# A two-layer mixer kernel: loops written out, Exps one head ahead, a new order at the program's head

## The chip, the cores and the metric

The kernel runs on one core of a Trainium2 chip. The metric is the device time of one execution, in microseconds (us), median of the runs shown. TensorE is called PE, its weight loads PEld, VectorE DVE, ScalarE ACT, GpSimd POOL; SP is the sync engine, which here only starts transfers.

## The reference

Two transformer-like blocks in float32 over 512 latent tokens (and 256 context tokens in the first), model width 2048:

```python
# first block
shift, scale, gate = split(silu(c) @ w_ada + b_ada, 3)
h  = rmsnorm(x, norm_g) * (1 + scale) + shift        # the same for ctx with c_ctx
u  = h @ w_in;  uc = hc @ w_in
ya = gdn_mixer(...)     # gated delta rule, 8 heads of 128, both directions
yb = rwkv_mixer(...)    # RWKV-7 recurrence, 16 heads of 64, both directions
x  = x + gate * (concat(ya, yb) @ w_out) -> rmsnorm
# delta rule, chunks of 64 (the kernel takes two as one unit of 128), state starts at zero
v_new = u_i - wk_i @ state
o_i   = q_i @ state + attn_i @ v_new
state = state * exp(gl_i) + k_i.T @ v_new
# second block: adaLN, attention in a window of 128, conformer convolution, w_out_2, layer norm
```

## The kernel before, in words

The program is a row of phases (PHASES), each with its own semaphores and with a barrier of all engines between two of them.

- phase_mod: the modulation c @ w_ada as 8 column groups of 512, two per round (groups), four rounds of 64 recorded matmuls each; the weights come in 1 MB slices through 8 slots that SP fills. Beside it the sum of squares of x and ctx: ACT squares hT (L253), PE sums over partitions with a matrix of ones (L289, L290), a pair of matmuls for each of 16 slices. Round 0 stands before the sums, rounds 1 to 3 behind them in a loop. DVE copies each round's result (L306, L308) and scales hT (L315).
- phase_gates: decay and beta of the delta rule, 32 columns; a long chain on DVE behind 32 matmuls.
- phase_split: ACT rounds hT to the multiplier's format (h_high, L1045), DVE makes the remainder (h_low, L1052).
- phase_proj: all columns of w_in.
- phase_rwkv: 8 pairs of heads. In each pair a scan over 2 x 6 steps with the preparation of the next half pair filled in between the steps (prepare), the finish of the pair before (heads_out) and the weighted sum of later w_ada slices on DVE (later, L2293, L2296). SP loops over pairs 0 to 6, PE and ACT over pairs 1 to 6, DVE over pairs 2 to 6. A loop's waits compare against a value that registers hold.
- phase_gdn: 8 heads. scan(m) does six steps j of head m; fill(m, n), n = 0 to 17, three per step, puts in the finish of head m-1 (norm), the second part of the preparation of head m+1 (invert) and the first part of head m+2 (start). start(a, 0): DVE takes differences of gates (L779, L782), ACT makes Relu and Exp of them (L707 to L710); start(a, 1): PE forms k k^T (L599), DVE multiplies it by those Exps (L788). In a step PE multiplies the state (L665), DVE subtracts (L867), PE multiplies by the inverse (L671), ACT copies (SA, L746), PE makes the state's increment (L675), DVE adds it (L873); steps 2 to 5 give an output (L683, L684, L885).
- phase_out and phase_two: output projection and the second block.

What each engine does is written out by hand in the order in which it runs; there is no scheduler. In phase_gdn, step 0 of each head starts from two memsets:

```python
for d in range(2):
    dve.memset(St[0][:, d], 0.0).then_inc(S["g_s"], 1)
```

Of the kernel before, what the change touches and what calls it, by code (L numbers as in the profile page):

```python
# [69 lines left out]
def program(nc, io, out):  # L70
    ctx = ExitStack()
    with ctx:
# [20 lines left out]
        mixers, halves_of_h = ctx.enter_context(ExitStack()), ctx.enter_context(ExitStack())  # L93
        first, work = ctx.enter_context(ExitStack()), ctx.enter_context(ExitStack())
# [71 lines left out]
        for f, prefixes in phases:  # L166
            at[0] = 0
            if prefixes == "s":
                first.close()
                env["high"] = sb("h_high", [P, KT, TOK], F32R, scope=halves_of_h)  # L170
                env["low"] = sb("h_low", [P, KT, TOK], F32R, scope=halves_of_h)
            if prefixes == "pq":
                mixers.close()
# [24 lines left out]
def phase_mod(nc, e):  # L198
# [10 lines left out]
    sq = carve(2, TOK)  # L209
    rstd = carve(TOK)  # L210
# [11 lines left out]
    with nc.Block() as block:  # L222
# [21 lines left out]
        def _(act):  # L244
            act.dma_start(hT[:, :, 0:LAT], io["xT"]).then_inc(S["a_x"], 16)
            act.dma_start(hT[:, :, LAT:TOK], io["ctxT"]).then_inc(S["a_x"], 16)
            act.wait_ge(S["a_par"], 48)
            act.activation(csg[:], pr("c", 3 * KT).rearrange("p (k s) -> p k s", s=3), ACT.Sigmoid).then_inc(S["a_sig"], 1)
            act.wait_ge(S["a_x"], 32)
            for k in range(KT):  # L250
                if k >= 2:
                    act.wait_ge(S["a_ss"], k - 1)
                act.activation(sq[:, k % 2], hT[:, k], ACT.Square).then_inc(S["a_sq"], 1)  # L253

            act.wait_ge(S["a_ss"], KT)
# [11 lines left out]
        def _(pe):  # L267
            pe.wait_ge(S["a_par"], 48)
            pe.wait_ge(S["a_cs"], 1)

            def groups(i):
# [9 lines left out]
                for b in range(2):  # L281
                    pe.wait_ge(S["a_row"], 1 + i * 2 + b + 1)
                    for n in range(4):
# [2889 lines left out]
```

## Time and profile before

| | |
|---|---|
| median of 3 runs | 4146.47 us (4146.44 to 4146.88) |
| profiled execution, its own time | 4150.37 us |
| its span, first to last instruction | 4148.6 us |
| mean granted TensorE clock | 0.921 |
| busy | PE 85%, PEld 71%, DVE 53%, ACT 25%, POOL 20% |
| DMA | 467.29 MB, mean 113 GB/s |

The span is the profiled execution's; its own time is 1.8 us more, and the median of the runs is 3.9 us below that. Busy shares are means over phases with different limits, so the chain in each phase has to be read by itself.

### The profile page before, as it was taken

The numbers are of one execution on the slowest core, as the hardware profiler recorded it, in microseconds if no ns is written. First come the engines' busy times: TensorE is split into PE (matmuls) and PEld (weight loads), VectorE is DVE, ScalarE is ACT, GpSimd is POOL, SyncE is SP. The second block draws the span as 40 slices with busy tenths as digits, with TensorE's granted clock in tenths as the row PEclk, the third lists the DMA queues.
The fourth block names the chain that finished last, engine by engine and source line by source line (L and its number), as shares of the span: only waits on it lengthen the run. The fifth ranks groups of instructions, "written<-read, shape, count | busy, mean of one in ns | idle before, by whom it ended". The sixth has DMA issues, their size and how long they took to land. (4 is left out here: it accounts for less than half of the span.)

```text
span 4148.6 us, 53353 instructions
## 1 busy us (share of the span) xinstructions
PE 3525.3 (85%) x19810; PEld 2930.3 (71%) x19810; DVE 2202.7 (53%) x4087; ACT 1042.4 (25%) x1716; POOL 825.8 (20%) x589
## 2 busy tenths in 40 slices
PE   6849999989999588888888778887797989887897
PEld 2138888878888487887788668776676777665484
DVE  0252655555545366666666646665103789993102
ACT  1122554543333112221221212221002221212102
POOL 0000000000000011111111100000575665563273
PEclk9969999999999799999999868888899999998899
DMA  6411434345455455555555333321523221121221
GB/s 270 132 44 64 138 121 148 121 136 174 151 167 167 94 125 127 127 116 118 123 124 119 107 94 107 103 81 66 191 81 117 71 71 61 66 71 46 101 96 66
DMA packets 409792, 467.29 MB, mean 113 GB/s; under 512 B 266544, under 2 KB 310416, under 8 KB 403040
## 3 DMA queue, kind: packets, MB, share of 16 engines
q1 hardware_dynamic: 377536, 379.20, 30.9%
q0 software_dynamic: 20480, 67.13, 5.4%
q10 hardware_dynamic: 11552, 17.95, 1.2%
q8 instruction: 144, 2.36, 0.2%
q14 instruction: 80, 0.66, 0.1%
HBM read 382.80 MB, written 83.99 MB: 113 GB/s over the span
## 5 line engine op out<-in xcount | busy, mean ns | idle before, releaser
L953 PE MATMUL pjl<-high,w_high 128*128 128x512 f32 x912 | 374.8, 411 | 48.4 <-DVE low L2519 16.3
L934 POOL TENSOR_TENSOR w_high<-ring_o,cst 128x1024 fp32r<-128x1024 f32 x152 | 302.2, 1988 | 491.9 <-PE pjl L955 343.0
L936 POOL TENSOR_TENSOR w_low<-ring_o,w_high 128x1024 fp32r<-128x1024 f32 x152 | 380.8, 2505 | 11.9
L954 PE MATMUL pjl<-low,w_high 128*128 128x512 f32 x912 | 365.9, 401 | 0.0
L955 PE MATMUL pjl<-high,w_low 128*128 128x512 f32 x912 | 364.1, 399 | 0.0
L2892 DVE SCALAR_TENSOR_TENSOR arena<-arena,par 128x512 f32<-128x512 f32 x232 | 312.5, 1347 | 7.4
L1931 POOL DMA_DIRECT2D arena_r<-in_w_ada x256 | 137.4, 537 | 857.0 <-DVE arena_r L2296 754.4
L953 PEld LDWEIGHTS pjl<-high,w_high 128*128 128x128 f32 x912 | 177.8, 195 | 103.6 <-issue 53.0
L1090 PE MATMUL pjl<-h_high,wh_in 128*128 128x512 f32 x544 | 214.8, 395 | 24.2 <-DVE wl_in L1109 24.2
L1109 DVE TENSOR_TENSOR wl_in<-ring,wh_in 128x1024 fp32r<-128x1024 f32 x136 | 164.2, 1221 | 132.6 <-ACT wh_in L1102 132.6
L1090 PE MATMUL xu<-h_high,wh_in 128*128 128x512 f32 x544 | 220.2, 405 | 0.0
L1925 POOL MEMSET unused<- 128x1 f32 x3 | 0.2, 98 | 1101.5 <-POOLq L194 1101.5
L1090 PE MATMUL xu<-h_high,wl_in 128*128 128x512 f32 x544 | 214.9, 395 | 0.0
L1090 PE MATMUL pjl<-h_high,wl_in 128*128 128x512 f32 x544 | 214.4, 394 | 0.0
L1090 PE MATMUL xu<-h_low,wh_in 128*128 128x512 f32 x544 | 213.9, 393 | 0.0
L1090 PE MATMUL pjl<-h_low,wh_in 128*128 128x512 f32 x544 | 213.5, 393 | 0.0
L955 PEld LDWEIGHTS pjl<-high,w_low 128*128 128x128 f32 x912 | 177.7, 195 | 38.8
L954 PEld LDWEIGHTS pjl<-low,w_high 128*128 128x128 f32 x912 | 177.8, 195 | 38.0 <-issue 1.9
L2296 DVE SCALAR_TENSOR_TENSOR arena_r<-arena_r,csk 128x512 f32 (+1 forms) x240 | 179.7, 749 | 13.4 <-DMA arena_r<-in_w_ada 2.3
L2088 PE MATMUL xu<-arena_r 128*128 128x128 f32 x384 | 90.5, 321 | 105.5 <-DVE arena_r L2316 78.0
L1102 ACT ACTIVATE wh_in<-ring 128x1024 fp32r<-128x1024 f32 x136 | 142.6, 1054 | 100.4 <-DMA ring<-in_w_lr 58.6
L2170 ACT ACTIVATE arena_r<-tp 128x384 f32<-128x384 f32 (+1 forms) x96 | 57.4, 598 | 402.8 <-PE tp L2047 402.0
(454 smaller groups left out, 7920.4 us busy)
## 6 DMA issues: line engine op xcount, KB each, us to landing
ring<-in_w_lr SPq DMA_DIRECT2D x136, 512.0 KB, 3.7
arena_r<-in_w_ada POOLq DMA_DIRECT2D x256, 256.0 KB, 3.2
arena<-in_w_ada SPq DMA_DIRECT2D x32, 1024.0 KB, 7.4
ring_o<-in_w_out SPq DMA_DIRECT2D x64, 512.0 KB, 3.8
ring_o<-in_w SPq DMA_DIRECT2D x64, 512.0 KB, 3.7
arena_r<-rk_d SPq DMA_DIRECT2D x128, 192.0 KB, 5.1
rk_d<-arena_p SPq DMA_DIRECT2D x72, 192.0 KB, 1.9
arena_p<-gate_rows SPq DMA_DIRECT2D x32, 386.0 KB, 6.1
```

Source lines behind the costliest of these rows:

```text
L934: pool.tensor_tensor(h, w, one, ALU.mult).then_inc(S[done + "h"], 1)
L936: pool.tensor_tensor(l, w, h.bitcast(F32), ALU.subtract).then_inc(w_used, 1)
L953: pe.matmul(lat, wh[:, c], ah, start=kk == 0, stop=False)
L954: pe.matmul(lat, wh[:, c], al, start=False, stop=False)
L955: last = pe.matmul(lat, wl[:, c], ah, start=False, stop=kk == KT - 1)
L1090: last = pe.matmul(lat, w[:, s, k], a[:, kk, 0:LAT], start=first, stop=final)
L1102: act.activation(e["wh"][:, n % RING], e["ring2"][:, n % 2], ACT.Copy).then_inc(S["p_hi"], 1)
L1109: dve.tensor_tensor(e["wl"][:, n % RING], e["ring2"][:, n % 2], e["wh"][:, n % RING].bitcast(F32), ALU.subtract).then_inc(S["p_split"], 1)
L1931: pool.dma_start(late[:, x % LATE], io["w_ada"][8 + x // 16, :, x % 16]).then_inc(S[f"r_lw{x % LATE}"], 16)
L2088: pe.matmul(xu[d][:, 0:P], LC[hh][:, d, u], twice(V[hh][:, d, u]), start=True, stop=False)
L2296: dve.scalar_tensor_tensor(a, late[:, k % LATE], c, a, ALU.mult, ALU.add).then_inc(S["r_lu"], 1)
L2892: link(dve.scalar_tensor_tensor(ca[:], x[:, o:o + LAT], w[:, o:o + 1], ca[:], ALU.mult, ALU.add))
```

## The change

- phase_mod: SP asks for par first, then four weight slices, then cst and rows; ACT makes the sigmoid of c before it starts the transfers of x and ctx. Rounds 0 and 1 of the modulation both stand ahead of the sums. The 16 squares are added up on DVE (adds, between the copies of round 1), and PE multiplies the total by ones once.
- phase_split is gone; its 16 ACT and 16 DVE instructions stand in phase_gates, ACT's behind the first Exp, DVE's behind the memsets.
- phase_rwkv: the loops of SP, PE, ACT and DVE are written out, so that addresses and waits are constants.
- phase_gdn: step 0 has no product with the state, no subtraction and no memset; its new state is a copy. Step 5 makes no new state. start(m+3, 0) is in scan m, on DVE at n = 15 and on ACT at n = 16, in place of start(m+2, 0) at n = 0; start(2, 0) stands ahead of the first scan.
- The block transfers (blocks_out to inverse_in) are as they were.

```diff
@@ phase_mod
             sp.dma_start(par[:], io["par"]).then_inc(S["a_par"], 16)
-            sp.dma_start(cst[:], io["cst"]).then_inc(S["a_par"], 16)
-            sp.dma_start(rows[:], io["rows"]).then_inc(S["a_par"], 16)
             for s in range(SLOTS):
...
+                if s == 3:
+                    sp.dma_start(cst[:], io["cst"]).then_inc(S["a_cst"], 16)
+                    sp.dma_start(rows[:], io["rows"]).then_inc(S["a_rows"], 16)
...
+            act.wait_ge(S["a_par"], 16)
+            act.activation(csg[:], pr("c", 3 * KT).rearrange("p (k s) -> p k s", s=3), ACT.Sigmoid).then_inc(S["a_sig"], 1)
             act.dma_start(hT[:, :, 0:LAT], io["xT"]).then_inc(S["a_x"], 16)
             act.dma_start(hT[:, :, LAT:TOK], io["ctxT"]).then_inc(S["a_x"], 16)
-            act.wait_ge(S["a_par"], 48)
-            act.activation(csg[:], pr("c", 3 * KT).rearrange("p (k s) -> p k s", s=3), ACT.Sigmoid).then_inc(S["a_sig"], 1)
+            act.wait_ge(S["a_rows"], 16)
...
-                    act.wait_ge(S["a_ss"], k - 1)
+                    act.wait_ge(S["a_add"], k - 1)
...
-            groups(0)
-            for k in range(KT):
-                pe.wait_ge(S["a_sq"], k + 1)
-                pe.matmul(ssl[:, 0:LAT], ones, sq[:, k % 2, 0:LAT], start=k == 0, stop=k == KT - 1)
-                pe.matmul(ssc[:, 0:CTX], ones, sq[:, k % 2, LAT:TOK], start=k == 0, stop=k == KT - 1).then_inc(S["a_ss"], 1)
-            with pe.Fori(1, GROUPS // 2) as i:
+            pe.wait_ge(S["a_zero"], 1)
+            groups(0, True)
+            groups(1)
+            pe.wait_ge(S["a_add"], KT)
+            pe.matmul(ssl[:, 0:LAT], ones, sums[:, 0:LAT], start=True, stop=True)
+            pe.matmul(ssc[:, 0:CTX], ones, sums[:, LAT:TOK], start=True, stop=True).then_inc(S["a_ss"], 1)
+            with pe.Fori(2, GROUPS // 2) as i:
                 groups(i)
...
+            def adds(k0, k1):
+
+                for k in range(k0, k1):
+                    dve.wait_ge(S["a_sq"], k + 1)
+                    if k:
+                        dve.wait_ge(S["a_add"], k)
+                        dve.tensor_tensor(sums[:], sums[:], sq[:, k % 2], ALU.add).then_inc(S["a_add"], 1)
...
                 for b in range(2):
+                    if i == 1:
+                        adds(*((0, 4), (4, KT))[b])
@@ phase_gates
+            for k in range(KT):
+                act.activation(high[:, k], hT[:, k], ACT.Copy).then_inc(S["b_h"], 1)
...
+            for k in range(KT):
+                dve.wait_ge(S["b_h"], k + 1)
+                dve.tensor_tensor(low[:, k], hT[:, k], high[:, k].bitcast(F32), ALU.subtract).then_inc(S["b_l"], 1)
+            dve.wait_ge(S["b_l"], KT)
             dve.wait_ge(S["b_y"], 2)
@@ phase_gdn, tensor: scan
-                        pe.wait_ge(S["g_s"], m * 14 + 2 * j + d + 1)
+                        if j == 0:
+                            break
+                        pe.wait_ge(S["g_s"], m * 10 + 2 * (j - 1) + d + 1)
...
-                        pe.matmul(xu[d][:, P:2 * P], TT[m % 2][:, d, G_ORDER[d][j]], W[:, d], start=True, stop=True).then_inc(S["g_sa"], 1)
+                        else:
+                            pe.wait_ge(S["g_wc"], m * 10 + 2 * (j - 1) + d + 1)
+                        pe.matmul(xu[d][:, P:2 * P], TT[m % 2][:, d, u], W[:, d] if j else bV[m % 2][:, d, u], start=True, stop=True).then_inc(S["g_sa"], 1)
...
+                        if j == UN - 1:
+                            continue
                         pe.matmul(xu[d][:, 2 * P:3 * P], KL[m % 2][:, d, G_ORDER[d][j]], SA[:, d], start=True, stop=True).then_inc(S["g_ds"], 1)
@@ phase_gdn, scalar: fill (vector: the same with n == G_EARLY, which is 15)
-                if m + 2 < GH:
+                if m + 2 < GH and n:
                     start(m + 2, n)
+                if m + 3 < GH and n == G_EARLY + 1:
+                    start(m + 3, 0)
@@ phase_gdn, vector: scan
-                if m:
-                    dve.wait_ge(S["g_s"], m * 14)
-                for d in range(2):
-                    dve.memset(St[0][:, d], 0.0).then_inc(S["g_s"], 1)
...
+                        if j == 0:
+                            dve.tensor_copy(new[:, d], xu[d][:, 2 * P:3 * P]).then_inc(S["g_s"], 1)
+                            continue
@@ phase_rwkv (PE; ACT, DVE and SP alike)
-            with pe.Fori(1, PAIRS - 1) as i:
+            for i in range(1, PAIRS - 1):
                 pair(i, True)
```

The order of instructions at three places. **PE at the program's head.** Before (the first rows, up to the loop over rounds 1 to 3, of which L278 is the body; the rows of L289 and L290 come 16 times), and then the change, where the modulation's lines are L283 and L291 and the sums' L297 and L298:

```order
L278 MATMUL xu<-arena 3x512 x32
L284 MATMUL tp<-cst,arena 128x128 x8
L289 MATMUL pjl<-arena,cst 128x512
L290 MATMUL pjc<-arena,cst 128x256
```

```order
L283 MATMUL xu<-arena 3x512 x32
L291 MATMUL tp<-cst,arena 128x128 x8
L283 MATMUL xu<-arena 3x512 x32
L291 MATMUL tp<-cst,arena 128x128 x8
L297 MATMUL pjl<-arena,cst 128x512
L298 MATMUL pjc<-arena,cst 128x256
```

A whole round has moved ahead of the sums, and the sums are one pair of matmuls.

**ACT in phase_gdn, from step 5 of one head to the preparation filled into the next.** Before: Square of norm (L726), Relu and Exps of start (L707 to L710), the copy SA of step 0 (L746), Sqrt of norm (L729), T's copies (L720).

```order
L746 ACTIVATE arena_r<-xu 128x128 x4
L726 ACTIVATE arena_r<-arena_r 128x512
L707 ACTIVATE arena_r<-arena_r 128x1536
L709 ACT_TABLE_LOAD
L709 ACTIVATE arena_r<-arena_r 128x1536
L710 ACTIVATE arena_r<-arena_r 128x12
L746 ACTIVATE arena_r<-xu 128x128 x2
L729 ACT_TABLE_LOAD
L729 ACTIVATE arena_r<-pjl,arena_r 128x512
L720 ACTIVATE arena_r<-tp 128x768 x2
```

Now (L743 to L746 are Relu and Exps, L762 the Square, L784 the copy, L765 the Sqrt, L756 T's copies):

```order
L784 ACTIVATE arena_r<-xu 128x128 x4
L743 ACTIVATE arena_r<-arena_r 128x1536
L745 ACT_TABLE_LOAD
L745 ACTIVATE arena_r<-arena_r 128x1536
L746 ACTIVATE arena_r<-arena_r 128x12
L762 ACTIVATE arena_r<-arena_r 128x512
L784 ACTIVATE arena_r<-xu 128x128 x2
L765 ACT_TABLE_LOAD
L765 ACTIVATE arena_r<-pjl,arena_r 128x512
L756 ACTIVATE arena_r<-tp 128x768 x2
```

The Exps stand ahead of the Square, and they are those of the head after the one that they were for.

**DVE at the same place.** Before: the last state (L873) and output (L885) of a head, the memsets (L861), step 0 (L867), invert (L811), the gates' differences (L779, L782), k k^T times the Exps (L788), the new state.

```order
L867 TENSOR_TENSOR arena_r<-arena_r,xu 128x128 x2
L873 SCALAR_TENSOR_TENSOR arena_r<-arena_r,xu 128x128 x2
L885 TENSOR_TENSOR arena_r<-arena_r,pjl 128x128 x2
L861 MEMSET arena_r 128x128 x2
L867 TENSOR_TENSOR arena_r<-arena_r,xu 128x128 x2
L811 TENSOR_TENSOR arena_r<-arena_r 128x768 x2
L779 TENSOR_TENSOR arena_r<-arena_r,gc 128x6x64 x2
L782 TENSOR_TENSOR arena_r<-arena_r,gc 128x6
L779 TENSOR_TENSOR arena_r<-arena_r,gc 128x6x64 x2
L782 TENSOR_TENSOR arena_r<-arena_r,gc 128x6
L788 TENSOR_TENSOR arena_r<-tp,arena_r 128x768 x2
L873 SCALAR_TENSOR_TENSOR arena_r<-arena_r,xu 128x128 x2
```

Now (L908 is the subtraction, L820 and L823 the differences, L931 the output, L852 invert, L829 the product with the Exps, L917 the copy that makes the state):

```order
L908 TENSOR_TENSOR arena_r<-arena_r,xu 128x128 x2
L820 TENSOR_TENSOR arena_r<-arena_r,gc 128x6x64 x2
L823 TENSOR_TENSOR arena_r<-arena_r,gc 128x6
L820 TENSOR_TENSOR arena_r<-arena_r,gc 128x6x64 x2
L823 TENSOR_TENSOR arena_r<-arena_r,gc 128x6
L931 TENSOR_TENSOR arena_r<-arena_r,pjl 128x128 x2
L852 TENSOR_TENSOR arena_r<-arena_r 128x768 x2
L829 TENSOR_TENSOR arena_r<-tp,arena_r 128x768 x2
L917 COPY arena_r<-xu 128x128 x2
```

The four differences have moved from behind step 0 of a head to step 5 of the head before.

## Rows read from the trace of the kernel before

**Rows 1.** Timeline of phase_mod: start us, us, engine, line, operation [idle before it].
```profile
1.47 17.54 ACTq L246 DMA_DIRECT2D hT<-in_ctxT  x1
20.93 29.65 PE L278 MATMUL xu<-arena 128*3 128x512 f32 x64 [20.93 <-DVE arena L299]
...
63.50 1.58 ACT L253 ACTIVATE arena<-hT 128x768 f32<-128x768 f32 x2 [42.91 <-DMA hT<-in_ctxT]
...
87.70 27.63 PE L278 MATMUL xu<-arena 128*3 128x512 f32 x64
...
173.24 0.66 PE L284 MATMUL tp<-cst,arena 128*128 128x128 f32 x4
```
**Rows 2.** DMA, 0 to 30 us: packets, MB, share; then issues, KB, us to landing.
```profile
q1 hardware_dynamic: 1261, 8.51, 70.3%
q10 hardware_dynamic: 1447, 2.96, 25.7%
...
par<-in_par SPq DMA_DIRECT2D x1, 402.0 KB, 3.2
```
**Rows 3.** Timeline of phase_gates, phase_split and the start of phase_proj.
```profile
224.15 0.55 DVE L420 TENSOR_SCALAR arena<-arena 16x772 f32<-16x772 f32 x1 [34.72 <-ACT arena L400]
...
260.15 11.84 ACT L1045 ACTIVATE h_high<-hT 128x768 fp32r<-128x768 f32 x16 [3.85 <-PEq L194]
261.02 13.99 DVE L1052 TENSOR_TENSOR h_low<-hT,h_high 128x768 fp32r<-128x768 f32 x16 [1.85 <-ACT h_high L1045]
...
275.91 0.26 POOL L1199 MEMSET unused<- 128x1 f32 x6 [275.06 <-POOLq L194]
```
**Rows 4.** DVE timeline, the first instruction of pairs 0, 1, 2, 3, 6, 7.
```profile
1442.04 0.19 DVE L2357 MEMSET arena_r<- 128x64 f32 x2
...
1558.02 0.18 DVE L2357 MEMSET arena_r<- 128x64 f32 x2
...
1676.88 0.19 DVE L2357 MEMSET arena_r<- 128x64 f32 x2
...
1799.77 0.19 DVE L2357 MEMSET arena_r<- 128x64 f32 x2 [3.25 <-issue]
...
2165.35 0.19 DVE L2357 MEMSET arena_r<- 128x64 f32 x2 [3.23 <-issue]
...
2283.76 0.18 DVE L2357 MEMSET arena_r<- 128x64 f32 x2
```
**Rows 5.** ACT timeline in phase_gdn, the start of a head.
```profile
2708.85 0.63 ACT L726 ACTIVATE arena_r<-arena_r 128x512 f32<-128x512 f32 x1 [2.88 <-DVE arena_r L885]
2713.95 1.48 ACT L707 ACTIVATE arena_r<-arena_r 128x1536 f32<-128x1536 f32 x1 [4.47 <-DVE arena_r L782]
...
2718.24 0.42 ACT L746 ACTIVATE arena_r<-xu 128x128 f32<-128x128 f32 x2
```
**Rows 6.** DVE timeline there, from step 5 of the head before.
```profile
2704.12 0.48 DVE L867 TENSOR_TENSOR arena_r<-arena_r,xu 128x128 f32<-128x128 f32 x2
...
2708.33 0.48 DVE L885 TENSOR_TENSOR arena_r<-arena_r,pjl 128x128 f32<-128x128 f32 x2 [1.12 <-PE pjl L684]
...
2711.81 1.02 DVE L779 TENSOR_TENSOR arena_r<-arena_r,gc 128x384 f32<-128x384 f32 x2
...
2720.10 0.60 DVE L873 SCALAR_TENSOR_TENSOR arena_r<-arena_r,xu 128x128 f32<-128x128 f32 x2
```
**Rows 7.** PE timeline there.
```profile
2710.57 1.02 PE L644 MATMUL pjl<-arena_r,cst 128*128 128x512 f32 x2
2711.43 2.84 PE L599 MATMUL tp<-arena_r 128*128 128x128 f32 x24
2718.55 1.22 PE L675 MATMUL xu<-arena_r 128*128 128x128 f32 x4 [4.28 <-ACT arena_r L746]
2720.24 2.08 PE L604 MATMUL tp<-arena_r 128*128 128x128 f32 x8 [0.47 <-DVE arena_r L788]
```
**Rows 8.** Window early in the head before: length, busy by engine, PEclk, DMA share, GB/s.
```profile
2664.00:2668.00 4.00, 3.53 (x16) 3.24 (x16) 3.56 (x7) 1.83 (x2) 0.00 (x0) 0.50 0.29 43
```

More of the change, by code:

```diff
@@ L93, in program @@
         mixers, halves_of_h = ctx.enter_context(ExitStack()), ctx.enter_context(ExitStack())
+        gates_work = ctx.enter_context(ExitStack())
         first, work = ctx.enter_context(ExitStack()), ctx.enter_context(ExitStack())
@@ L209, in phase_mod @@
     sq = carve(2, TOK)
+    sums = carve(TOK)
     rstd = carve(TOK)
@@ L267, in _, with groups @@
         def _(pe):
-            pe.wait_ge(S["a_par"], 48)
             pe.wait_ge(S["a_cs"], 1)
-            def groups(i):
+            def groups(i, first=False):
                 for b in range(2):
@@ L282, in groups @@
                     pe.wait_ge(S["a_row"], 1 + i * 2 + b + 1)
+                    if first and b == 0:
+                        pe.wait_ge(S["a_cst"], 16)
                     for n in range(4):
@@ L295, in _ @@
         def _(dve):
-            dve.memset(modr[:], 0.0).then_inc(e["w_used"], RING)
+            dve.memset(modr[:], 0.0).then_inc(S["a_zero"], 1)
+            dve.wait_ge(S["a_zero"], 1)
+            dve.memset(sums[:], 0.0).then_inc(e["w_used"], RING)
             dve.memset(eps[:], 1e-6).then_inc(S["a_eps"], 1)
@@ L350, in phase_gates @@
     ea = carve(1)
-    gc = e["gc"]
+    gc, high, low = e["gc"], e["high"], e["low"]
     R = slice(0, 16)
@@ L479 @@
 G_TURNED, G_DONE = 6, 10
+G_EARLY = 15
 def phase_gdn(nc, e):
@@ L755, in _ @@
                 invert(0, n)
+            start(2, 0)
             for m in range(GH):
@@ L850, in fill @@
                     invert(m + 1, n)
-                if m + 2 < GH:
+                if m + 2 < GH and n:
                     start(m + 2, n)
+                if m + 3 < GH and n == G_EARLY:
+                    start(m + 3, 0)
                 if m + 1 < GH and n >= 3:
@@ L865, in scan @@
                     for d in range(2):
-                        dve.wait_ge(S["g_w"], m * 12 + 2 * j + d + 1)
+                        if j == 0:
+                            break
+                        dve.wait_ge(S["g_w"], m * 10 + 2 * (j - 1) + d + 1)
                         dve.tensor_tensor(W[:, d], bV[m % 2][:, d, G_ORDER[d][j]], xu[d][:, 0:P], ALU.subtract).then_inc(S["g_wc"], 1)
@@ L871, in scan @@
                         u = G_ORDER[d][j]
-                        dve.wait_ge(S["g_ds"], m * 12 + 2 * j + d + 1)
+                        if j == UN - 1:
+                            break
+                        dve.wait_ge(S["g_ds"], m * 10 + 2 * j + d + 1)
+                        if j == 0:
+                            dve.tensor_copy(new[:, d], xu[d][:, 2 * P:3 * P]).then_inc(S["g_s"], 1)
+                            continue
                         dve.scalar_tensor_tensor(new[:, d], old[:, d], egl[m % 2][:, d, u:u + 1], xu[d][:, 2 * P:3 * P],
@@ L897, in _ @@
                 invert(0, n) if n >= 3 else None
+            start(2, 0)
             dve.wait_ge(S["g_sh"], 1)
@@ L1035, in step_blocks @@
     dve.tensor_tensor(z[:, k + 1:16, 0:w], z[:, k + 1:16, 0:w], t, ALU.subtract).then_inc(S[q + "_z"], 1)
-def phase_split(nc, e):
-    hT, high, low, S = e["hT"], e["high"], e["low"], e["S"]
-    with nc.Block() as block:
-        @block.scalar
-        def _(act):
-            for k in range(KT):
-                act.activation(high[:, k], hT[:, k], ACT.Copy).then_inc(S["s_h"], 1)
-            act.wait_ge(S["s_h"], KT)
-        @block.vector
-        def _(dve):
-            for k in range(KT):
-                dve.wait_ge(S["s_h"], k + 1)
-                dve.tensor_tensor(low[:, k], hT[:, k], high[:, k].bitcast(F32), ALU.subtract).then_inc(S["s_l"], 1)
-            dve.wait_ge(S["s_l"], KT)
 def r_slots(d, hh):
@@ L1983, in _ @@
             load_a(0, 1)
-            with sp.Fori(0, PAIRS - 1) as i:
+            for i in range(PAIRS - 1):
                 blocks_there(i * 2 + 1)
@@ L2213, in _ @@
             pair(0, True, True)
-            with act.Fori(1, PAIRS - 1) as i:
+            for i in range(1, PAIRS - 1):
                 pair(i, True)
@@ L2285, in later @@
             def later(i, hh, n):
-                g, which = i * 2 + hh, 0 if isinstance(i, int) and i < 2 else 2
+                g, which = i * 2 + hh, 0 if i < 2 else 2
                 at = sum(LATER.get(q, 0) for q in range(n))
@@ L2375, in _ @@
             pair(0, True, True)
-            pair(1, True)
-            done = n_[0]
-            with dve.Fori(2, PAIRS - 1) as i:
-                n_[0] = 0
-                base[0] = done + (i - 2) * io["DV_R"]
+            for i in range(1, PAIRS - 1):
                 pair(i, True)
-                e["counts"]["DV_R"] = n_[0]
-            n_[0] = 0
-            base[0] = done + (PAIRS - 3) * io["DV_R"]
             pair(PAIRS - 1, False)
@@ L3170 @@
 ARENA = 32584
+GATES = 11264
 WORK, CORE = 14608, 49440
```

25 lines of the change are left out of this document (15 added, 10 removed).

## The prediction

> **What bounds the kernel now.** I read the page first (PE 85% busy, DVE 53%), then the phases one by one, since the change touches four of them and no other. In phase_mod the timeline shows PE at work from 20.93 us, at rest from about 51, waiting for x and ctx until 63.5, in the sums until 87.7, then three rounds of modulation without a break until 173.24 [rows 1]. So PE's order sets the end, and what PE does while it waits is free. PE starts at 20.93 because the sigmoid of c stands in ACT's queue behind the start of two transfers, the second of which holds the queue for 17.54 us [rows 1]. phase_split has PE idle: 15.8 us from ACT's first rounding (260.15) to the first instruction of phase_proj (275.91) [rows 3]. In phase_rwkv the seven full pairs are read from the first DVE instruction of each [rows 4]: pair 0 takes 116.0 us (no loop but SP's, and no heads_out), pair 1 118.9 (loops on PE, ACT and SP), pair 2 122.9, pairs 3 to 5 121.9 each ((2165.35 - 1799.77) / 3), pair 6 118.4. Every start behind a jump back of DVE's loop has an idle time of 3.2 us put down to issue; pair 7, where the loop is left, has none [rows 4]. In phase_gdn a head's start is a chain: gate differences on DVE, Relu and Exps on ACT, 4.3 us (2713.95 to 2718.24), then SA, then PE, idle for 4.28 us until then [rows 5, 7], then the state at 2720.10 [rows 6]. The granted clock is then low (0.50, its level of 1.2 GHz, in [rows 8], the same place one head earlier), and 8 products take 2.08 us where 24 took 2.84 before the idle time [rows 7].
>
> **Head of the program.** par lands 3.2 us after its issue [rows 2], at about 4; with the sigmoid and one product PE could begin at 5, and the first weight slice, which shares the queue with par alone, should be there by 6. PE starts 15 us sooner. Two rounds now run before the sums; a round takes (173.24 - 87.70) / 3 = 28.5 us, so they end at 6 + 57 + 2 = 65, the 2 for a start at the low clock. The transfers bound this too: 16 slices of 1.05 MB, par, cst, x and ctx are 24.6 MB, and 11.5 MB moved in the first 30 us, some 0.4 MB per us once they run [rows 2]: 63 us. Of these bytes the ACT queue got 2.96 MB against 8.51 of SP's [rows 2], and x and ctx took from 1.47 to 63.5 [rows 1]. They start 4 us later and SP's queue stays full, so I put them at 67. The 16 squares then go at the pace of DVE's additions, 13.99 / 16 = 0.87 [rows 3] plus a hand-over, 0.95: 84. Copy, transposes and the one pair of sums at low clock take 4: round 2 starts at 88, where round 1 started at 87.7. One round is saved, 28.5, less 0.3 and less 2 for the cold start: **-26**. If the later x costs 8 us more it is -18, if SP's queue yields, -29. DVE's reciprocal and eight scalings (about 12 us) stay inside round 2.
>
> **phase_split.** 15.8 us go. Its work moves behind a wait in phase_gates: DVE stands idle 34.72 us before L420 [rows 3], and 13.99 us of subtractions one step behind 11.84 us of ACT fit in; without that cover they would cost those 14. **-16** (-15 to -16.5).
>
> **Loops written out.** The four jumps back of DVE (behind pairs 2 to 5) cost the difference between 121.9 to 122.9 and pair 6's 118.4: 3.5 to 4.5 each, 14.9 together. PE's own jumps lie mostly beside it. Here the Trainium skill speaks against the change: Advanced Engine Details and Errata, Control Flow Timing, gives a compare-and-branch some 108 ns. By that page the four would give 0.4 us and not 14.9. The idle time of 3.25 us in the trace decides. Its page Runtime: NRT & Kernel Launch, Instruction fetch mechanics, has the other rule, that a taken branch out of the loaded code stalls until the target's page is there. What is left is the register work of the waits. Pair 1, whose DVE is written out, is no faster than pair 6, whose DVE is not, so DVE's is hidden; PE's could be at most the 118.4 - 116.0 that separate pair 6 from pair 0, which also lacks heads_out. I take 118.0 for a written-out pair: (2283.76 - 1558.02) - 6 x 118.0 = **-18**; at 118.4 -15, at 116.0 -30. If a written-out stream brought stalls of its own it would be less, -12.
>
> **Delta rule.** With the rows I lay out a head's start anew. Step 5's subtraction ends at 2704.6; the differences (2711.81 to 2713.95, 2.1 us) follow at once and end at 2706.7 [rows 5, 6]. Their G was loaded long before. They stand in a gap, since step 5's state update is gone, and the output L885 is not later than its 2708.33. ACT does Relu and Exps from 2706.8 to 2711.1, and only then the Square (0.63), which PE's product with ones awaits, and behind that product stands L599, which needs 2.84 us at full clock [rows 5, 7]. So: Square done 2711.7, SA 2712.2, ones 2712.7, L599 2715.5, increment and state at 2716.6, against 2720.10: 3.5 us sooner. But PE has then been idle for some 3.5 us, against 4.28 before, and may run L599 at the low clock, about 5.5 us: state at 2719.3, 0.8 sooner. In either case the slow stretch begins 6 us earlier and ends earlier, which puts up to 6 us of PE's work back to the full level and is worth up to 3. I take 4 us for each of the heads 0 to 5, which have Exps, and 1.5 for heads 6 and 7, which lose only memset, two products and a subtraction: 24 + 3 = **-27**. Ends: 1 us each, -8; 7 us each, -45.
>
> **Sum.** -26 - 16 - 18 - 27 = -87. The profiled execution took 4150.4 us, so 4063.4; the median of the runs stands 3.9 below it: **4059.5 us**.
>
> **Rivals.**
> - *The Square behind the Exps*, 0.14: in the delta rule the wait only changes its name, PE waits for the Square instead of SA and L599 runs slow. For it: the order on ACT and the low clock after the idle time [rows 7, 8]. Against: the whole chain starts 7 us sooner. Delta rule -8: 4078.5.
> - *The clock stays up*, 0.12: the idle time becomes short enough, the slow start of every head goes. For it: one idle time of 4.28 us is all that stands ahead of the slow start [rows 7]. Against: 3.5 us of it are still there. Delta rule -45: 4041.5.
> - *Loops written out bring nothing*, 0.05: pairs wait for loads or for DVE and stay at 121. Against: pair 6 has the same work in 118.4. Without the 18: 4077.5.
> - *x and ctx starve*, 0.04: SP's queue is served far ahead of ACT's while PE eats slices earlier; round 2 starts 8 us later or more: 4067.5 and up.
> - *Slower, by code loading*, 0.02: each written-out pair stops as often as code must be fetched, 3.25 us each time [rows 4]. Six pairs must lose the other 69 us (26 + 16 + 27), which takes 69 / (6 x 3.25) = 3.5 stops in a pair; from there on the kernel is slower. With six in a pair: 4146.5 - 69 + 117 = 4194.5. Against: pair 0 stands written out on PE, ACT and DVE and shows nothing of it in its 116.0 us.
>
> **How the numbers follow.** The forecast has 0.63. Its own range, from the ends of the head and of the pairs with 3 to 6 us a head in the delta rule, is 4045 to 4073. The range of eight in ten has to reach into the first two rivals, whose centres are 4078.5 and 4041.5: 4038 to 4083. A difference from no change that a measurement can tell is 0.2%, 8 us. All cases but the last are faster by more than that: 0.97 faster, 0.01 same, 0.02 slower.
>
> **What would show it.** Right: PE's first product at 6 us and third round at 88; phase_gates unchanged in length and followed by phase_proj at once; pairs 1 to 6 all within 1 us of 118 with no idle time put down to issue at their start; PE's wait at a head's start put down to the Square, shorter than 4.28 us, and a head's period shorter by about 4. Wrong: a third round later than 92; additions that hold up round 1's copy beyond 85; pairs of different length, which would mean that loads or code set them; a head's period shorter by less than 2 or by more than 6, in which case the clock is what I misjudged.

## The result, and the profile after

| | before | after |
|---|---|---|
| median of 4 runs each, same chip | 4146.68 us (4146.44 to 4152.31) | 4082.9 us (4077.84 to 4089.93) |
| ratio | 1 | 0.9844, 95% interval 0.9827 to 0.9861 |
| profiled execution, its span | 4150.4, 4148.6 | 4083.69, 4081.7 |
| mean granted clock of PE | | 0.926 |

The kernel is 64 us faster, where 87 were forecast. The length of each phase, from its first instruction to the first one of the next phase (us), against the terms of the sum:

| | phase_mod | gates + split | phase_proj | phase_rwkv | phase_gdn | phase_out | phase_two |
|---|---|---|---|---|---|---|---|
| before | 187.3 | 87.9 | 1101.7 | 1017.6 | 498.1 | 294.8 | 960.4 |
| after | 178.2 | 72.3 | 1102.9 | 1004.4 | 472.8 | 293.7 | 956.6 |
| measured | -9.1 | -15.6 | +1.2 | -13.2 | -25.3 | -1.1 | -3.8 |
| forecast | -26 | -16 | 0 | -18 | -27 | 0 | 0 |

So one term failed by 17 us, one by 5, and two held. phase_two, which the change doesn't touch, lies between 955.7 and 960.8 in the eleven profiles of the experiments below: its 3.8 us are no effect of the change. For the small terms this table is a better measure than the medians.

**Head of the program.** PE's timeline from the start, which answers to [rows 1]:

```profile
7.92 30.19 PE L283 MATMUL xu<-arena 128*3 128x512 f32 x64 [7.92 <-DMA arena<-in_w_ada]
...
39.47 27.63 PE L283 MATMUL xu<-arena 128*3 128x512 f32 x64
89.97 1.11 PE L291 MATMUL tp<-cst,arena 128*128 128x128 f32 x4 [22.87 <-DVE arena L329]
103.11 1.11 PE L291 MATMUL tp<-cst,arena 128*128 128x128 f32 x4 [12.03 <-DVE arena L329]
104.02 1.91 PE L297 MATMUL pjl<-arena,cst 128*128 128x512 f32 x2
...
106.71 5.79 PE L283 MATMUL xu<-arena 128*3 128x512 f32 x11
```

PE starts 13 us sooner and both rounds end at 67.1 (39.47 + 27.63), 2 later than I wrote. Then it stands for 22.87 us and once more for 12.03, both put down to DVE's copies of the second round's two halves (L329), between which the additions stand. The third round begins at 106.71, not at 88. The ACT timeline says what DVE waited for:

```profile
3.74 0.24 ACT L251 ACTIVATE arena<-par 128x48 f32<-128x48 f32 x1 [1.70 <-DMA par<-in_par]
...
4.47 23.48 ACTq L253 DMA_DIRECT2D hT<-in_ctxT  x1
84.63 2.31 ACT L259 ACTIVATE arena<-hT 128x768 f32<-128x768 f32 x3 [80.64 <-DMA hT<-in_ctxT]
...
88.29 0.84 ACT L259 ACTIVATE arena<-hT 128x768 f32<-128x768 f32 x1 [0.22 <-DVE arena L319]
89.36 0.85 ACT L259 ACTIVATE arena<-hT 128x768 f32<-128x768 f32 x1 [0.22 <-DVE arena L319]
```

ctx is there at 84.6, though its transfer was started at 4.47. The DMA view over 0 to 90 us (queue, packets, MB, share; then issues with KB and median us to landing) shows the two queues; q1 is SP's, q10 ACT's:

```profile
q1 hardware_dynamic: 3776, 26.75, 72.5%
q10 hardware_dynamic: 4128, 6.29, 19.1%
...
arena<-in_w_ada SPq DMA_DIRECT2D x24, 1024.0 KB, 18.8
...
hT<-in_ctxT ACTq DMA_DIRECT2D x1, 2048.0 KB, 80.1
```

24 slices went through before ctx was complete: the eight of the third round too, which PE could not touch before the sums. SP asks for a slice as soon as PE has used the one in its place, so a PE that starts sooner keeps SP's queue full. How the two queues share shows best where both have work all the time, from 60 to 80 us (the same view of that stretch):

```profile
q1 hardware_dynamic: 985, 7.23, 87.8%
q10 hardware_dynamic: 983, 1.01, 14.7%
```

The packets are as many on one queue as on the other, and SP's hold 7.3 KB each where ctx's hold 1 KB. So SP's queue gets seven times the bytes, and ctx comes at 0.05 MB per us. Left alone (60 to 64 us in the first experiment below) it moves 963 packets, 0.97 MB, at five times that rate. From one square to the next also takes longer than planned: 89.36 - 88.29 = 1.07 us, not 0.95. A square waits until the addition of the last but one is done (0.22 of idle time), and DVE adds without a break, 12 additions in 12.62 us (1.05 each), where I had taken 0.87.

**phase_split** is gone: POOL's memset, the first instruction of phase_proj, stands at 251.27, right behind a phase_gates that is as long with this work in it as it was without (72.3 us, before 72.1), and ACT's 16 roundings lie where planned, beside DVE's wait:

```profile
180.37 11.82 ACT L417 ACTIVATE h_high<-hT 128x768 fp32r<-128x768 f32 x16
...
251.27 0.26 POOL L1228 MEMSET unused<- 128x1 f32 x6 [250.42 <-POOLq L197]
```

**Loops.** DVE's first instruction of pair 3 in the timeline has lost its 3.25 us of issue [rows 4]:

```profile
1770.24 0.74 DVE L2324 SCALAR_TENSOR_TENSOR arena_r<-arena_r,csk 128x512 f32<-128x512 f32 x1
1770.95 0.19 DVE L2385 MEMSET arena_r<- 128x64 f32 x2
```

From such rows pair 0 takes 116.15 us and pairs 1 to 6 take 119.07, 119.33, 118.87, 117.96, 119.07 and 119.74, 714.0 in all, against 725.7 before. They are even, as forecast, but at 119.0 and not at 118.0.

**Delta rule.** A head's start in PE's timeline, which answers to [rows 7], and in ACT's [rows 5]:

```profile
2654.34 0.61 PE L705 MATMUL xu<-arena_r 128*128 128x128 f32 x4
2659.41 2.07 PE L674 MATMUL pjl<-arena_r,cst 128*128 128x512 f32 x2 [4.45 <-ACT arena_r L762]
2661.27 4.70 PE L629 MATMUL tp<-arena_r 128*128 128x128 f32 x24
2665.81 0.61 PE L711 MATMUL xu<-arena_r 128*128 128x128 f32 x4
2667.02 1.16 PE L634 MATMUL tp<-arena_r 128*128 128x128 f32 x8 [0.60 <-DVE arena_r L829]
```
```profile
2654.45 1.48 ACT L743 ACTIVATE arena_r<-arena_r 128x1536 f32<-128x1536 f32 x1 [1.18 <-DVE arena_r L823]
...
2657.25 1.48 ACT L745 ACTIVATE arena_r<-arena_r 128x1536 f32<-128x1536 f32 x1
2658.64 0.20 ACT L746 ACTIVATE arena_r<-arena_r 128x12 f32<-128x12 f32 x1
2658.74 0.61 ACT L762 ACTIVATE arena_r<-arena_r 128x512 f32<-128x512 f32 x1
```

PE's wait is as long as before (4.45 against 4.28) and now carries the name of the Square (L762), which stands behind Relu, Exp and tail on ACT. The 24 products behind it take 4.70 us, where before they took 2.84 ahead of the wait. But the 8 products of L634 take 1.16 us and not 2.08: the low clock comes earlier and ends earlier. The windows of the two kernels show it (length, busy by engine, PEclk, DMA share, GB/s). First the changed kernel, whose SA of this head starts at 2659.26:

```profile
2658.00:2662.00 4.00, 2.59 (x6) 1.56 (x7) 0.00 (x0) 3.45 (x7) 0.00 (x0) 0.54 0.02 4
2662.00:2666.00 4.00, 4.00 (x24) 4.00 (x24) 0.96 (x1) 0.20 (x1) 0.00 (x0) 0.61 0.00 0
2666.00:2670.00 4.00, 2.02 (x16) 1.64 (x15) 3.92 (x8) 0.00 (x0) 0.00 (x0) 1.00 0.34 51
```

Then the kernel before, the two windows that follow [rows 8], where SA of that head started at 2663.42:

```profile
2668.00:2672.00 4.00, 3.40 (x17) 3.11 (x17) 3.94 (x7) 1.00 (x2) 0.00 (x0) 0.50 0.56 78
2672.00:2676.00 4.00, 4.00 (x30) 4.00 (x30) 1.56 (x3) 0.96 (x3) 0.00 (x0) 0.78 0.90 353
```

In a steady head the granted clock is at its lower level (1.2 GHz) for 6.9 us (2658.3 to 2665.2), where it was for 13.6 (3.4 and 10.2 us in one period of 54.7). It ends 5.9 us behind SA now and ended 10.4 us behind it before. The period is 51.0 us.

### The profile page after: what moved, and what is told of

It reads as the page before. It is cut to its first block and busy times, and to the rows that moved or that the text cites. A ratio compares the mean times of both kernels' runs of the same rounds, so it can differ in the third digit from the quotient of the medians.

```text
span 4081.7 us, 50949 instructions
## 1 busy us (share of the span) xinstructions
PE 3465.7 (85%) x19686; PEld 2881.3 (71%) x19686; DVE 2204.9 (54%) x4056; ACT 1041.4 (26%) x1716; POOL 824.9 (20%) x589
## 5 line engine op out<-in xcount | busy, mean ns | idle before, releaser
L2324 DVE SCALAR_TENSOR_TENSOR arena_r<-arena_r,csk 128x512 f32<-128x512 f32 x240 | 179.6, 748 | 13.6 <-DMA arena_r<-in_w_ada 2.8
L2117 PE MATMUL xu<-arena_r 128*128 128x128 f32 x384 | 88.1, 315 | 105.5 <-DVE arena_r L2344 92.7
```

The lines of the kernel that those rows point to most:

```text
L2117: pe.matmul(xu[d][:, 0:P], LC[hh][:, d, u], twice(V[hh][:, d, u]), start=True, stop=False)
L2324: dve.scalar_tensor_tensor(a, late[:, k % LATE], c, a, ALU.mult, ALU.add).then_inc(S["r_lu"], 1)
```

## The experiments

Three questions were open: whether ctx is late because SP's queue runs ahead, what of the 25 us in the delta rule comes from which of its two edits, and which engine's loop the 13 us of phase_rwkv belong to. All runs were timed beside the kernel before on the same chip; its medians there were 4142.53 us (the three kernels of the program's head and the split Exps), 4144.09 (Exps back, DVE's loop, PE's loop, the best) and 4143.52 (the zero state's work back, ACT's and SP's loops, the changed kernel again).

### Slices of the third round behind x and ctx

```diff
-            with sp.Fori(1, GROUPS // 2) as i:
+            for i in range(1, GROUPS // 2):
+                if i == 2:
+                    sp.wait_ge(S["a_x"], 32)
                 for s in range(SLOTS):
```

> The changed kernel, but SP asks for round 2's weight slices of the modulation only when x and ctx are in. Theory 1 (x and ctx starve: they landed at 84.5 us because SP's queue always had eight slices waiting, those of round 2 too, and got the larger share): all bytes up to round 1 are 24.6 MB at some 0.41 MB per us, so x and ctx land at 63 to 67, the squares end 19 us after that, round 2 starts near 87 and not at 106.7, phase_mod ends near 158 and not at 177.9, and the whole takes 16 to 20 us less than the changed kernel. Rival (ACT's queue is slow by itself at some 75 to 80 GB/s, whatever SP's does): x and ctx still land at 80 or later, and less than 4 us are gained.

Measured: 4061.31 us, ratio 0.9795 (0.9772 to 0.9817). ACT's and PE's timelines:

```profile
64.93 2.31 ACT L260 ACTIVATE arena<-hT 128x768 f32<-128x768 f32 x3 [60.74 <-DMA hT<-in_ctxT]
```
```profile
83.42 1.11 PE L292 MATMUL tp<-cst,arena 128*128 128x128 f32 x4 [12.03 <-DVE arena L330]
...
86.80 25.48 PE L284 MATMUL xu<-arena 128*3 128x512 f32 x59
```

ctx lands 19.7 us sooner and the third round begins 19.9 sooner, at 86.80, within 1.2 of the 88 of my forecast; phase_mod is 157.4 us long, 20.8 less. SP's loop is written out here as well; what that does by itself was not tried, but ctx's earlier landing accounts for the gain. phase_mod is now 29.9 us shorter than before, where I had forecast 26: the late ctx was all that the head term lacked.

### The sums behind the third round instead

```diff
             groups(1)
+            groups(2)
             pe.wait_ge(S["a_add"], KT)
...
-                    if i == 1:
-                        adds(*((0, 4), (4, KT))[b])
+                    if i == 2 and b == 1:
+                        adds(0, 10)
...
+                if i == 2:
+                    adds(10, KT)
```

> The changed kernel with the sum of squares between rounds 2 and 3 of the modulation instead of between 1 and 2. Theory 1 (PE's idle time from 67 to 103 us is all that the late x costs): round 2 runs from 67 to 96 while x and ctx land near 85, the additions end near 102.5, round 3 starts near 106 and phase_mod ends near 149 with 29 us less than 177.9. Rival (the additions on DVE or a slower x under more weights set the end): x lands after 90 and less than 20 us are gained.

Measured: 4067.48 us, ratio 0.9817 (0.9791 to 0.9842); phase_mod 160.2. ACT's timeline:

```profile
97.84 2.31 ACT L259 ACTIVATE arena<-hT 128x768 f32<-128x768 f32 x3 [93.82 <-DMA hT<-in_ctxT]
```

PE now works through three rounds without a break, and ctx comes at 97.8: the more slices PE uses before the sums, the later the transfer that was started at 4.5 us. PE then still stands for 13.28 and 5.06 us ahead of the sums. 18 us come back, and the rival's reading (x after 90, less than 20 gained) is the right one.

### Both

```diff
+                if i == 2:
+                    sp.wait_ge(S["a_x"], 32)
...
+            groups(2)
             pe.wait_ge(S["a_add"], KT)
```

> Both edits. Theory 1: x and ctx in at 63 to 67, squares done by 85 beside round 2, which runs from 68 to 98 since its weights are asked for at 64; sums at 98, round 3 to 130, phase_mod ends near 143, 35 us less than 177.9. Rival (round 2 now waits for its weights, which come at the pace of the transfers): round 2 ends after 103, phase_mod after 148.

Measured: 4061.94 us, ratio 0.9804 (0.9781 to 0.9826); phase_mod 149.5. ctx lands at 64.8, but DVE's first addition stands behind its copy of the third round's first half (L330), so it begins at 84.93, 20 us after the data are there:

```profile
83.68 0.68 DVE L330 COPY arena<-xu 3x512 f32<-3x512 f32 x1 [16.05 <-PE xu L284]
...
84.93 9.46 DVE L320 TENSOR_TENSOR arena<-arena 128x768 f32<-128x768 f32 x9
```

PE waits 5.52 us ahead of the sums. The phase ends at 150.3, later than the theory's 143 and where the rival had it, but not for the rival's reason: the third round ends at 97.4, as the theory said. That the phase is 8 us shorter and the median no better than in the first experiment is no contradiction: phase_rwkv took 1006.5 us in this profile against 1001.9, and the intervals overlap. The place of the additions was my mistake; it is mended in the last kernel.

### Exps split into two parts

A head's start was PE waiting for the Square behind Relu and Exps. Here the differences go to step 12 on DVE, Relu and Exp to step 13 on ACT, and only the small tail stays at steps 15 and 16.

```diff
+G_DIFF = 12
...
-                if m + 3 < GH and n == G_EARLY + 1:
+                if m + 3 < GH and n == G_DIFF + 1:
                     start(m + 3, 0)
+                if m + 3 < GH and n == G_EARLY + 1:
+                    start(m + 3, -1)
```

> The changed kernel; the gate differences for ET stand at n = 12 on DVE and their Relu and Exp at n = 13 on ACT, only the small tail difference and its Exp stay at n = 15 and 16. Theory 1 (at a head's start PE waits for the Square, which stands behind 4.3 us of Exps on ACT): PE's wait of 4.45 us shrinks to about 1, the clock stays at its full level there, and a head's period goes from 51.0 to 45 to 47, so 5 x 4 to 5 x 6 = 20 to 30 us less. Rival (the wait only moves: DVE is late at n = 12 or the Square is then late for its output): period 49 or more, less than 10 us.

Measured: 4059.19 us, ratio 0.9787 (0.9763 to 0.981); phase_gdn 445.0, 27.8 less than after. PE's timeline of a head's start, and the window there:

```profile
2594.04 0.61 PE L706 MATMUL xu<-arena_r 128*128 128x128 f32 x4
2595.45 1.13 PE L675 MATMUL pjl<-arena_r,cst 128*128 128x512 f32 x2 [0.79 <-ACT arena_r L765]
2596.41 2.84 PE L630 MATMUL tp<-arena_r 128*128 128x128 f32 x24
```
```profile
2598.00:2602.00 4.00, 3.30 (x28) 2.92 (x26) 3.60 (x7) 0.00 (x0) 0.00 (x0) 1.00 0.15 24
```

The wait falls from 4.45 to 0.79 us, the clock stays at its upper level, the 24 products take 2.84 us again, and the period is 44.65 us in four of the five periods behind the first (in the other one the clock was at its lower level for 5.6 us, and it took 46.58). So the Square behind the Exps was a real wait and the clock fell behind it, as two of the rivals had it.

### Exps back, the zero state's work left out

```diff
-                if m + 2 < GH and n:
+                if m + 2 < GH:
                     start(m + 2, n)
-                if m + 3 < GH and n == G_EARLY:
-                    start(m + 3, 0)
...
-            start(2, 0)
```

> The changed kernel with the gate differences, Relu and Exps of a head back at step 0 of the scan two heads ahead, as before the change; the products with the zero state stay away. Theory (the 25 us of the delta rule come from the Exps that now stand ahead of the head's start; the removed memset, two products and subtraction of a head lie beside other work): phase_gdn 472.8 -> 488 to 494, a head's period 51.0 -> 53 to 54.3, PE's idle time at a head's start longer than in the changed kernel. Rival (the zero state brought it, since it stood in the same chain): phase_gdn stays at 473 to 478, period 51 to 51.7.

Measured: 4093.99 us, ratio 0.9879 (0.9863 to 0.9896); phase_gdn 481.6. That is between the two readings and nearer to the rival's. PE's timeline of a head's start:

```profile
2661.83 2.84 PE L629 MATMUL tp<-arena_r 128*128 128x128 f32 x24
2668.54 1.22 PE L711 MATMUL xu<-arena_r 128*128 128x128 f32 x4 [3.87 <-ACT arena_r L782]
2670.24 2.08 PE L634 MATMUL tp<-arena_r 128*128 128x128 f32 x8 [0.47 <-DVE arena_r L826]
```

The pattern of before is all there [rows 7], wait and slow products included, but from step 5's subtraction (2657.05) to the new state (2670.10) 13.05 us pass, where before 15.98 did (2704.12 to 2720.10 [rows 6]). Those 2.93 us are gained ahead of the gate differences, which begin 4.76 us behind the subtraction (2661.81) and began 7.69 us behind it before (2711.81); from there on the two run alike. Step 5's products for a state that nobody reads took 1.22 us of a slow PE and held up the output (L885), and the memset and step 0's subtraction stood behind that output in DVE's queue: all of it did lie on that path.

### The zero state's work back, the Exps early

```diff
+                if m:
+                    dve.wait_ge(S["g_s"], m * 14)
+                for d in range(2):
+                    dve.memset(St[0][:, d], 0.0).then_inc(S["g_s"], 1)
...
-                        if j == 0:
-                            break
-                        pe.wait_ge(S["g_s"], m * 10 + 2 * (j - 1) + d + 1)
+                        pe.wait_ge(S["g_s"], m * 14 + 2 * j + d + 1)
```

> The changed kernel with the memsets, the two products with the zero state and their subtractions at a head's start restored (and the last state update of a head, which nobody reads); the early Exps stay. The kernel with only the zero state's work removed had phase_gdn 481.6 against 498.1 before and 472.8 in the changed kernel, so the zero state's share was 16.5 where the prediction gave it 3. Theory (the two parts work on one quantity, the length of the disturbed stretch at a head's start and the low clock behind it, so the second one applied is worth less than the first: the Exps moved alone bring 15 to 20 of the 25): phase_gdn 478 to 483. Rival (the parts add up: Exps 9, zero state 16.5): phase_gdn 489 to 490.

Measured: 4086.01 us, ratio 0.9866 (0.9849 to 0.9883); phase_gdn 476.0. That is 2 us below the theory's 478 to 483 and 13 below the rival's sum of the parts. The four kernels together, from the first SA of head 0 to that of head 7, with the time in between at which the granted clock was at its lower level:

| | zero state's work in | zero state's work out |
|---|---|---|
| Exps at step 0 | 360.5 us, 82.1 low | 342.8 us, 76.6 low |
| Exps early | 340.1 us, 40.4 low | 336.0 us, 45.9 low |

Each edit alone brings 18 to 20 us, and the second one 4 to 7. The other three cells are of one profile each; that of the changed kernel can be checked, since seven more profiles have the same phase_gdn: 332.3 to 336.6 us. With the lowest of them the second edit brings 7.8 to 10.5, still far from 18 to 20. With the Exps early, the steady period is 51.0 us with the zero state's work or without, and outside the spread of those profiles only the last two periods differ clearly (48.81 and 41.52 against 47.47 and 39.62). Leaving the zero state's work out shortens the path and hardly the low stretch (5.5 us less). Moving the Exps halves the low stretch, and half of the 41.7 us, 20.8, is about the 20.4 that it brought. But that is no rule: in the other column the same move takes 30.7 us from the low stretch and brings 6.8. How the two edits combine was measured, not explained step by step.

### Loops, one engine at a time

DVE's loop restored, all others written out:

> The changed kernel with VectorE's loop over pairs 2 to 6 of phase_rwkv restored, and all other loops written out. Theory (VectorE's jumps back were the cost, four of them, each some 3.8 us from the compare-and-branch to the next instruction): pairs 2 to 5 become 122 to 123 us long, pair 1 and 6 stay at 119, phase_rwkv 1004.4 -> 1016 to 1019, the kernel 12 to 15 us slower than the changed one. Rival (the jumps of PE, ACT and SP stood in the same chain and VectorE's alone hides among the written-out engines' slack): phase_rwkv +0 to +4.

PE's alone:

> The changed kernel with TensorE's loop over pairs 1 to 6 of phase_rwkv restored alone. Theory (TensorE's jumps lie beside VectorE's work at a pair's start): phase_rwkv 1004.4 -> 1004 to 1007, pairs 119 to 119.5. Rival (each of its 5 jumps back costs its 3.3 to 3.9 us): phase_rwkv 1020 to 1024, pairs 2 to 6 at 122.5.

ACT's and SP's:

> The changed kernel with the loops of ACT and of the DMA queue SP in phase_rwkv restored, those of PE and DVE written out. PE's loop alone brought the pairs 1 to 6 from 714.0 to 725.9 us, which is all that the loops before had cost (725.7), DVE's alone 722.5. Theory (ACT and SP have idle time at their jumps): pairs 1 to 6 at 712 to 717, phase_rwkv 1001 to 1006, within 4 us of the changed kernel. Rival (any engine's jump holds up the chain, since each pair hands work round between all of them): pairs 1 to 6 at 720 to 726.

The edit is the loop's one line, as here for PE; DVE's begins at pair 2, with its waits counted from a base in a register, as before:

```diff
-            for i in range(1, PAIRS - 1):
+            with pe.Fori(1, PAIRS - 1) as i:
                 pair(i, True)
```

The changed kernel was also run once more on another chip, as the measure for such small differences:

> The changed kernel once more, on another chip: how far its time and its stages move without any edit, as the measure for the small differences of the loop experiments. Expected: ratio 0.983 to 0.986, phase_mod 178, phase_rwkv 1001 to 1005, phase_gdn 469 to 473.

| loops in phase_rwkv | ratio (interval) | median, us | phase_rwkv, us | pairs 1 to 6, us |
|---|---|---|---|---|
| all (before) | 1 | 4146.68 | 1017.6 | 725.7 |
| none (after) | 0.9844 (0.9827 to 0.9861) | 4082.9 | 1004.4 | 714.0 |
| none, again | 0.9846 (0.9829 to 0.9862) | 4077.92 | 1006.9 | 715.8 |
| DVE | 0.9864 (0.9847 to 0.988) | 4088.28 | 1011.7 | 722.5 |
| PE | 0.9874 (0.9858 to 0.9891) | 4094.89 | 1019.6 | 725.8 |
| ACT and SP | 0.9855 (0.9839 to 0.9872) | 4082.68 | 1000.7 | 710.5 |

By the ratios alone the intervals overlap; the pairs decide. Nine profiles have no loop in this phase (the changed kernel twice and the seven experiments on the head, the delta rule and the best), and their pairs 1 to 6 take 711.2 to 715.8 us; DVE's 722.5 and PE's 725.8 lie clear of that, ACT's and SP's 710.5 just below. PE's loop by itself costs all that the loops of before cost, 11.8 us, DVE's by itself 8.5, and both together no more than PE's alone. The trace of the kernel before shows why: PE's compare-and-branch between pairs 2 and 3 lasts from 1793.66 to 1797.00, DVE's next instruction comes at 1799.77 [rows 4], and PE waits for that one. The two stops fall together. So DVE's theory held in part (8.5 for 12 to 15), and PE's fell: its rival was nearly right (1019.6 for 1020 to 1024). It is the jump that costs and not the waits' values in registers: with PE's loop, the 61st product of a pair comes 9.6 to 12.4 us behind DVE's memset, 8.1 without, and this lag grows no more up to the 481st. Behind pair 0, where PE does not jump, it is 8.0. Why the first products behind the jump lose more than the 0.5 to 1.1 us by which they start later is not shown in full; the clock is at its lower level for 92.2 us of these pairs, where the two profiles of the changed kernel have 78.5 and 85.3. The next rows show the stops themselves, PE's weight loads in the kernel with PE's loop and DVE's first instruction of a pair in the one with DVE's loop. Both have idle time put down to issue (the weight load L2117 has 1.84 us of it without a loop too, where it waits for the memset; DVE's has none):

```profile
1768.88 1.34 PEld L2076 LDWEIGHTS tp<-cst,arena_r 128*128 128x128 f32 x12
1773.19 0.30 PEld L2117 LDWEIGHTS xu<-arena_r 128*128 128x128 f32 x2 [2.97 <-issue]
```
```profile
1892.64 0.19 DVE L2386 MEMSET arena_r<- 128x64 f32 x2 [3.25 <-issue]
```

PE's product (L2117) starts at 1773.20, 1.36 us after the memset that it needs (1771.84 in that kernel), where without a loop it follows 0.26 us behind it (1771.21 behind 1770.95).

### The best of it together

Split Exps, slices of the third round behind x and ctx, sums behind the third round, and all 16 additions ahead of the third round's first copy.

```diff
-                    if i == 2 and b == 1:
-                        adds(0, 10)
+                    if i == 2 and b == 0:
+                        adds(0, KT)
```

> The changed kernel with the split Exps, with the request for the third round's slices behind the arrival of x and ctx, and with the sums behind the third round; all 16 additions now stand ahead of the third round's first copy, so that they run from about 66 to 83 us, before that copy is due at 83.7. Theory: TensorE waits 0 to 1 us ahead of the sums instead of 5.5; phase_mod ends at 143 to 145 us (149.2 in both_head, 177.9 in the changed kernel), phase_gdn 445, the kernel 60 to 63 us faster than the changed one: 4020 to 4025 us. Rival (the end of phase_mod is set by the scalings and the last round's copy chain, or slices for the last round come later since copies are late): phase_mod ends at 148 or later, 4026 to 4032.

Measured: 4023.87 us (4021.57 to 4030.86), ratio 0.9705 (0.9689 to 0.9721), 59 us faster than the changed kernel by the first of its two medians, 54 by the second. phase_mod 143.1, phase_gdn 448.0. DVE's and PE's timelines:

```profile
68.05 15.84 DVE L320 TENSOR_TENSOR arena<-arena 128x768 f32<-128x768 f32 x15
85.18 0.68 DVE L330 COPY arena<-xu 3x512 f32<-3x512 f32 x1 [1.30 <-PE xu L284]
```
```profile
69.72 29.16 PE L284 MATMUL xu<-arena 128*3 128x512 f32 x64 [2.46 <-DMA arena<-in_w_ada]
...
100.14 1.02 PE L299 MATMUL pjl<-arena,cst 128*128 128x512 f32 x2
101.00 0.59 PE L300 MATMUL pjc<-arena,cst 128*128 128x256 f32 x2
101.53 10.89 PE L284 MATMUL xu<-arena 128*3 128x512 f32 x25
```

PE's only idle time over 0.2 us between the rounds is 2.46 us for slices that were asked for after ctx, and the sums run at full clock in 1.4 us (100.14 to 101.53), where they took 2.7 behind an idle PE (104.02 to 106.71).

## Why the prediction was right or wrong

- **The sign, the range.** 4082.9 is inside 4038 to 4083, at its very edge, and 23 us above the forecast; the forecast's own range ended at 4073. That it falls inside at all is luck, by 0.1 us: the range reached so far for the sake of a rival about the delta rule, and the miss is at the program's head. The case that came true is one I had given 0.04, "x and ctx starve", from 4067.5 upward.
- **Head of the program, -26: mis-sized, -9.** The step that failed is "They start 4 us later and SP's queue stays full, so I put them at 67". I took the bytes of two rounds, x and ctx as one sum to be moved, 63 us, and did not ask what else stands in SP's queue by then. The third round's eight slices were in it, since SP asks when a place is free and not when PE will need it: ctx at 84.6. Asked for behind ctx, they leave it at 64.9, and the third round begins where I had it (86.80). I also read only the bytes of [rows 2]: its packets, 1261 of SP's queue and 1447 of ACT's, already showed that the queues take turns by packets and not by bytes, so that ctx with its small ones comes last as long as SP has slices to ask for. Two smaller misses: the first product at 7.92 instead of 6, because the first slice landed at 7.8 (6.6 to 7.3 in the four experiments on the head), and 1.07 us for a square instead of 0.95.
- **phase_split, -16: right.** Gates and split together lost 15.6 us, and the subtractions found their cover.
- **Loops, -18: the mechanism was right, its seat and size were not.** The idle time at a jump back was the cost, and the 108 ns of the Trainium skill (Advanced Engine Details and Errata, Control Flow Timing) are far from it: 3.3 to 3.9 us pass in PE's compare-and-branch and 3.5 to 3.9 us from DVE's to the engine's next operation, at every jump back over a pair. "PE's own jumps lie mostly beside it" is true of the kernel before, where they end while PE waits for DVE, but it says nothing of their price: alone they cost 11.8 us, DVE's alone 8.5. And 118.0 for a pair was too low; it came from halving the way to pair 0 without a row for it. Pair 0 stays 3 us shorter with no loop anywhere, so that difference isn't the loops'. The other 118.4 of [rows 4], pair 6, would have given 15; measured are 11.7 in the pairs and 13.2 in the phase.
- **Delta rule, -27: right in its sum, wrong in its parts.** Measured -25.3 (-28.4 in the second profile). I gave 24 to the Exps and 3 to the zero state. Alone they are worth 20.4 and 17.7 (22.1 and 16.5 by the length of the phase), and together 24.5. That the sum came out is luck: the zero state's work was put far too low, and the two don't add up, which the sum had no term for. What I wrote for the Exps, that the low stretch begins and ends earlier, is what the trace shows; but the wait did not shrink from 4.28 to 3.5 us, it is 4.45 and belongs to the Square. The slow variant of my path, a state 15.2 us behind step 5's subtraction, is the one that came true: 14.95 (2651.93 to 2666.88). The rival of the Square (0.14) was right on the wait and wrong on its price: it gave -8. And the rival "the clock stays up" (0.12) described what the split Exps then did: phase_gdn 53 us below before, where I had given it 45.
- **Code loading, slower: did not happen.** DVE's first instruction of pairs 1 to 6 has no idle time ahead of it, and PE's first product there waits 1.63 us, put down to DVE's memset. The stops that the traces do show are at the loops' jumps.

## What to carry to other kernels

A transfer that was started first isn't there first: when an engine upstream gets faster, ask what the other queues will now request ahead of the late one, and hold back requests whose data can't be used yet (here one wait on SP gave 20.8 us). A gap that several engines share is paid once by the longest: undo it on all of them or expect little, and test each alone before naming the one that costs. The price of an idle TensorE is the wait and the low clock behind it; two edits on the same path don't add up, and here the one that brought the wait under a microsecond was worth most (27.8 us on top of both).

## What the runs showed of the hardware

- Two queues that both have work take turns by packets, not by age and not by bytes: 985 packets of SP's queue and 983 of ACT's in the changed kernel from 60 to 80 us, 7.23 MB against 1.01. So ACT's ctx, 2 MB started at about 4.5 us, was complete at 84.5, 97.8 or 64.8 us, by how many slices SP's queue was given in the meantime. Over 90 us SP's queue moved 26.75 MB in 3776 packets, ACT's 6.29 MB in 4128.
- A jump back over a pair costs PE 3.3 to 3.9 and DVE 3.5 to 3.9 us, while on ACT, whose pair has 53 instructions and not PE's 824 or DVE's 238, the next register operation follows 0.25 us behind the branch (1770.71 to 1770.96 in the kernel with ACT's loop). Where a loop is left and the branch not taken, PE's takes 0.08 us and DVE's 0.06. That agrees with the rule of the Trainium skill (Runtime: NRT & Kernel Launch, Instruction fetch mechanics) on jumps out of the loaded code; no run here varied the length alone, so that it is the length and not the engine stays unshown, and from which length on it costs was not tried.
- With the split Exps, four of the five periods behind the first took 44.65 us, with 0 to 1.2 us at the lower clock, and the one with 5.6 us at it took 46.58. In the best kernel it was the same once (46.55 with 5.6 us). So here a third of the time at the lower level was lost, where moving the Exps alone brought back half of it.
